# Token halves at a tile's end, and a later fetch of the first rows of sums, in a two-layer hybrid diffusion kernel

## What is computed

```python
DEPTH, SEQ, CTX_LEN, D_MODEL = 2, 512, 256, 1024
PEER_HEADS, N_KEYS, N_EXPERTS, PEER_TOPK, PEER_BLOCK = 8, 128, 128 * 128, 16, 128

def peer(h, w_q, sub_keys, u_tab, v_tab):
    b, L, _ = h.shape
    q = (h @ w_q).reshape(b, L, PEER_HEADS, 2, D_HALF)
    scores = jnp.einsum("blhtd,htkd->blhtk", q, sub_keys)
    ...                 # top 16 of both key halves, top 16 of their sums
    gate = jax.nn.softmax(top_s.astype(jnp.float32), axis=-1).astype(h.dtype)
    ...
    def experts(args):  # blocks of 128 tokens, 8 heads x 16 experts each
        xt, it, gt = args
        act = jax.nn.gelu(jnp.einsum("tkd,td->tk", u_tab[it], xt))
        return jnp.einsum("tk,tkd->td", gt * act, v_tab[it])
    ...

def reference(...):
    for l in range(DEPTH):
        mod = (silu_c @ w_mod[l] + b_mod[l])[:, None, :]   # conditioning
        ...             # context: projection, bidirectional scan, final states
        ...             # latent: projection, pooling, bidirectional scan, mixing
        x = layer_norm(DEEPNORM_ALPHA * x + g1 * mix, ln_g[l, 0], ln_b[l, 0])
        h2 = x * (1 + sc2) + sh2
        x = layer_norm(DEEPNORM_ALPHA * x + g2 * peer(h2, ...), ln_g[l, 1], ln_b[l, 1])
        if not last:
            ...         # the same mixing and peer() for the context tokens
    return x
```

## Time and profile before

| | us |
|---|---|
| median of 3 runs | 4668.28 |
| lowest and highest run | 4664.34, 4676.31 |
| the profiled execution's own time | 4667.22 |
| its span in the trace | 4665.4 |

### The profile page before, as it was taken

One profiled execution on the slowest core, in us unless ns is written; L12 is line 12 of the kernel. 1 busy time (PEld: TensorE's weight loads), 2 busy tenths in 40 slices (PEclk: granted clock), 3 DMA queues, 4 the chain that ended last, 5 costly groups with the idle time before them and its releaser, 6 DMA issues. The chain is left out here.

```text
span 4665.4 us, 48881 instructions
## 1 busy us (share of the span) xinstructions
PE 3434.4 (74%) x15768; PEld 1728.3 (37%) x15768; DVE 3191.9 (68%) x6618; ACT 1543.8 (33%) x3799; POOL 2058.5 (44%) x1555
## 2 busy tenths in 40 slices
PE   7898889897799886555777557888997555655554
PEld 6586224332575333111333114767632111111111
DVE  5465887664766767766766776686666677777775
ACT  4442344343442225222222323474222222222221
POOL 0173444543123554555444551034355555555554
PEclk9899999999899989777789788999998777777778
DMA  5647999999647999999999995263699999999998
GB/s 212 218 158 298 410 410 395 420 423 393 232 161 272 422 417 398 409 421 421 398 425 425 391 412 211 101 204 109 236 423 413 416 412 423 414 408 414 411 418 361
DMA packets 276276, 1622.97 MB, mean 348 GB/s; under 512 B 47074, under 2 KB 61218, under 8 KB 87717
## 3 DMA queue, kind: packets, MB, share of 16 engines
q0 software_dynamic: 184320, 1342.26, 69.6%
q1 hardware_dynamic: 91700, 277.59, 16.3%
HBM read 1598.40 MB, written 21.33 MB: 347 GB/s over the span
## 5 line engine op out<-in xcount | busy, mean ns | idle before, releaser
L2727 PE MATMUL banks<-arena 128*64 128x512 f32 x5120 | 1569.3, 748 | 1003.2 <-ACT arena L2483 1001.8
L2193 POOL DMA_INDIRECT arena<-in_experts,arena x1280 | 1527.0, 1193 | 1660.0 <-PE banks L2727 1408.3
L2316 DVE CUSTOM_DVE_ANT_0 arena<-arena,token_copies 128x1024 f32<-128x1024 f32 x1280 | 1638.4, 1297 | 741.7 <-DMA arena<-in_experts,arena 681.6
L2727 PEld LDWEIGHTS banks<-arena 128*64 128x64 f32 x5120 | 377.1, 163 | 1983.4 <-ACT arena L2483 1357.0
L2476 ACT ACTIVATE arena<-arena 128x2 f32<-128x2 f32 x640 | 131.2, 205 | 1747.2 <-DVE arena L2316 1746.1
L2483 ACT ACTIVATE arena<-arena 128x64 f32<-128x64 f32 x1280 | 376.0, 340 | 298.8 <-POOL arena L2014 257.9
L303 POOL TENSOR_TENSOR wide_low<-wide_blocks,wide_high 128x1024 fp32r<-128x1024 f32 x88 | 219.1, 2513 | 277.7 <-ACT wide_high L292 233.3
L2540 PE MATMUL banks<-arena,wide_blocks 128*128 128x512 f32 (+3 forms) x960 | 307.0, 467 | 3.5 <-ACT arena L2345 2.1
L1025 POOL TENSOR_TENSOR arena<-arena 128x1024 f32<-128x1024 f32 x20 | 43.3, 2191 | 530.4 <-POOLq L853 479.5
L2617 PE MATMUL banks<-arena,wide_blocks 128*128 128x512 f32 x576 | 277.2, 619 | 0.0
L347 PE MATMUL banks<-activation_a,wide_high 128*128 128x256 f32 (+1 forms) x768 | 255.9, 333 | 23.8 <-DVE arena L1462 10.4
(11 more groups left out here) (268 smaller groups left out, 4789.0 us busy)
## 6 DMA issues: line engine op xcount, KB each, us to landing
wide_blocks<-in_wide SPq DMA_DIRECT2D x186, 1024.0 KB, 6.0
arena<-cum_rows SPq DMA_DIRECT2D x80, 256.0 KB, 3.8
arena<-in_experts,arena POOLq DMA_INDIRECT x1280, 11.1
pre_scan<-arena SPq DMA_DIRECT2D x16, 256.0 KB, 7.3
arena<-pre_scan SPq DMA_DIRECT2D x16, 256.0 KB, 5.2
residual<-in_tokens SPq DMA_DIRECT2D x6, 512.0 KB, 6.4
arena<-mod_rows SPq DMA_DIRECT2D x6, 512.0 KB, 8.5
norm_rows<-in_keys SPq DMA_DIRECT2D x3, 1024.0 KB, 6.5
```

The lines of the kernel that those rows point to most:

```text
L2193: pool.indirect_dma_start(out=v.ring[:, g % RING], out_offset=None, in_=io["experts"], in_offset=bass.IndirectOffsetOnAxis(ap=c.idx[:, u % ...
L2316: last = nc.vector.tensor_tensor_reduce(out=u_row, in0=u_row, in1=k.copies[:, n % NJ], scale=1.0, scalar=0.0, op0=ALU.mult, op1=ALU.add, a ...
L2727: mm = nc.tensor.matmul(k.ps[j * QUAD:(j + 1) * QUAD, a + half], v.lhs[:, g % 4, j], v.ring[:, (g * NJ + j) % RING, D + half * BANK:D + (h ...
```

## The change

**Row order.** At the seven tile ends, the last unit of the old tile and the first of the new one (14 of 80 units) take all eight rows of half 0 first and then all eight of half 1 (`row_of`). The other units are as before. Masks, gather indices, token copies and matmul targets follow `row_of`; the flags that start and stop an accumulation go by half. The copies of half 0 are made after the fourth group of the last unit, where VectorE has done the old tile's half 0, and those of half 1 after the last group. In the border units the two rows of a group therefore belong to the same half, and all four matmuls of a group write the same 64 output partitions.

**Rows of sums.** SyncE issues conditioning blocks up to half of the stage's count plus three, instead of two plus three, before it fetches the four tiles of rows, and ScalarE's two `unit_decays` come two turns later.

```diff
@@ -859,7 +859,7 @@
             if mods:
-                load_wides(k, sp, w0 + 2 + WIDE_SLOTS)
+                load_wides(k, sp, w0 + mods.count // 2 + WIDE_SLOTS)
             if rows:
@@ -908,8 +908,9 @@
                 mods.take(act, i)
-                if rows and i - turns // 2 in range(EARLY_UNITS):
-                    unit_decays(k, act, v, i - turns // 2, 0, 0, i - turns // 2, row0)
+                n = i - turns // 2 - 2
+                if rows and n in range(EARLY_UNITS):
+                    unit_decays(k, act, v, n, 0, 0, n, row0)
             if rows and not mods:
@@ -2074,6 +2075,17 @@
     dot_at = lambda g: FIRST + 22.0 + ROW * g
+    def row_of(u, n):
+        border = (u % PEER_HEADS == 0 and u) or (u % PEER_HEADS == PEER_HEADS - 1 and u < UNITS - 1)
+        return (n % RANKS, n // RANKS) if border else (n // NJ, n % NJ)
+    def first_of_half(u, n):
+        return all(row_of(u, x)[1] != row_of(u, n)[1] for x in range(n))
+    def last_of_half(u, n):
+        return all(row_of(u, x)[1] != row_of(u, n)[1] for x in range(n + 1, TOPK))
     PRE, ITEM = proj_at(N) + 8.0, (8.0 if short else 13.0)
@@ -2084,7 +2096,8 @@
     kept_before = lambda e: sum(1 for x in range(e) if keep_of(x) == keep_of(e))
-    copy_at = lambda n: FIRST + 13.0 + 3.0 * n if n < 2 * NJ else dot_at(n // (2 * NJ) * PEER_HEADS * TOPK - 1) + 5.0
+    copy_at = lambda n: (FIRST + 13.0 + 3.0 * n if n < 2 * NJ else
+                         dot_at(n // (2 * NJ) * PEER_HEADS * TOPK - 1 - (RANKS if n // 2 % NJ == 0 else 0)) + 5.0)
     first_two = (2 if ahead else 1) if short else 1 if not ahead else NT
@@ -2179,6 +2192,11 @@
         def _(pool):
+            def row_index(u, n):
+                q, j = row_of(u, n)
+                return c.idx[:, u % 4, q, j:j + 1]
             def gather():
@@ -2192,7 +2210,7 @@
                             out=v.ring[:, g % RING], out_offset=None, in_=io["experts"],
-                            in_offset=bass.IndirectOffsetOnAxis(ap=c.idx[:, u % 4, n // NJ, n % NJ:n % NJ + 1], axis=0),
+                            in_offset=bass.IndirectOffsetOnAxis(ap=row_index(u, n), axis=0),
                         ).then_inc(k.landed[g % RING].sem, 16)
@@ -2307,14 +2325,15 @@
                         yield dot_at(g)
-                        if u % PEER_HEADS == 0 and n < NJ:
-                            dve.wait_ge(k.copy_ready.sem, k.copy_ready.at(t * 2 * NJ + 2 * n + 2))
+                        j = row_of(u, n)[1]
+                        if u % PEER_HEADS == 0 and first_of_half(u, n):
+                            dve.wait_ge(k.copy_ready.sem, k.copy_ready.at(t * 2 * NJ + 2 * j + 2))
                         dve.wait_ge(k.landed[g % RING].sem, r0 + 16 * (g // RING + 1))
...
                         last = nc.vector.tensor_tensor_reduce(
-                            out=u_row, in0=u_row, in1=k.copies[:, n % NJ], scale=1.0, scalar=0.0,
+                            out=u_row, in0=u_row, in1=k.copies[:, j], scale=1.0, scalar=0.0,
                             op0=ALU.mult, op1=ALU.add, accum_out=c.act_in[:, g % 32:g % 32 + 1])
@@ -2446,15 +2465,15 @@
 
-            def copies(t):
-                for j in range(NJ):
+            def copies(t, part):
+                for j in part:
                     for half in range(2):
...
                         if t >= 1:
-                            act.wait_ge(k.dots.sem, b0["dots"] + t * PEER_HEADS * RANKS)
+                            act.wait_ge(k.dots.sem, b0["dots"] + t * PEER_HEADS * RANKS - (RANKS // 2 if j == 0 else 0))
                         nc.scalar.copy(k.copies[:, j, half * BANK:(half + 1) * BANK],
@@ -2463,7 +2482,7 @@
                 c.take_gates(act, 0)
-                yield from copies(0)
+                yield from copies(0, range(NJ))
                 yield FIRST + 13.0 + 8.0
@@ -2480,15 +2499,16 @@
                         for j in range(NJ):
-                            last = nc.scalar.activation(v.lhs[:, g % 4, j], c.masked[:, q * NJ + j], ACT.Copy,
+                            rank, part = row_of(u, q * NJ + j)
+                            last = nc.scalar.activation(v.lhs[:, g % 4, j], c.masked[:, rank * NJ + part], ACT.Copy,
                                                         scale=c.gel[:, a + j:a + j + 1])
...
                             c.softmax(act, u + 2)
-                    if u % PEER_HEADS == PEER_HEADS - 1 and t + 1 < NT:
-                        yield from copies(t + 1)
+                        if u % PEER_HEADS == PEER_HEADS - 1 and t + 1 < NT and q % (RANKS // 2) == RANKS // 2 - 1:
+                            yield from copies(t + 1, [q // (RANKS // 2)])
                     if u % PEER_HEADS == 1 and t >= 1:
@@ -2684,13 +2704,13 @@
 
-            def copies(t):
-                if t == 1:
+            def copies(t, part):
+                if t == 1 and 0 in part:
                     pe.wait_ge(k.s_copied.sem, nth(k.s_copied, N))
-                if t == first_two and ahead and short:
+                if t == first_two and ahead and short and 0 in part:
                     pe.wait_ge(k.pre["evac"].sem, pre0["evac"] + ITEMS)
-                for j in range(NJ):
+                for j in part:
                     for half in range(2):
@@ -2724,19 +2744,24 @@
                             for j in range(NJ):
+                                n = q * NJ + j
+                                part = row_of(u, n)[1]
                                 mm = nc.tensor.matmul(
-                                    k.ps[j * QUAD:(j + 1) * QUAD, a + half], v.lhs[:, g % 4, j],
+                                    k.ps[part * QUAD:(part + 1) * QUAD, a + half], v.lhs[:, g % 4, j],
                                     v.ring[:, (g * NJ + j) % RING, D + half * BANK:D + (half + 1) * BANK],
-                                    start=(first and q == 0), stop=(final and q == RANKS - 1), skip_group_check=True)
+                                    start=(first and first_of_half(u, n)), stop=(final and last_of_half(u, n)),
+                                    skip_group_check=True)
                         mm.then_inc(k.slot_free.sem, 1)
...
                             c.spread(pe, u + 1)
+                        if final and t + 1 < NT and q == RANKS // 2 - 1:
+                            yield from copies(t + 1, [0])
                     if final:
...
                         if t + 1 < NT:
-                            yield from copies(t + 1)
+                            yield from copies(t + 1, [1])
 
...
     k.loaded.advance(64)

```

## The result

The changed kernel takes 4716.12 us, the median of nine runs (4689.21 to 4726.12), against 4667.29 us for nine runs of the kernel before. The ratio is 1.0101, its 95% interval 1.0086 to 1.0116: by the ratio 47 us more (40 to 54). I had forecast 4675 and a range up to 4700. The side on which the sum lay was right; the size was not.

What follows compares the result with a forecast made beforehand. The DMA engines were taken as the bound in retrieval. Terms -8 + 9 + 2 + 6 - 2 = +7 us on 4667.2 gave 4674, and 4675 as the profiled execution lies 1 us below the median; range 4652 to 4700.

Steps and rivals of the forecast that it cites:

- the hidden rival: Lengthened groups cost nothing, because matmuls of one half overlap or the queue takes it all: about 4652 us; chance 0.22.
- The third rival: A group's eight weight loads, 163 ns each, no longer run beside the other half's matmuls: about 4710 us; chance 0.06.
- -8: Six latent tile ends: removing the bubbles gives back 8.1 us at best, bounds 0 and 12.3.
- part 1: Bubbles at the seven tile ends: the wait for token copies is covered twice over; removing them gives at most 17.8 us.
- The fourth rival: Half 0's copies come late because TensorE's list reaches them late, and the wait returns: 4680 us; chance 0.04.
- The rival with TensorE as the bound in the latent units: Groups of layers 0 and 1, at half clock: 58 us a unit that now takes 40; 4704 us; chance 0.18.
- the 199 us: TensorE in the 14 border units: 1.78 us more for each of 112 same-half groups at the full clock.
- Context, +9: Context's two border units: 122.6 us of TensorE work in 105, less queue and small gaps: +9 us, +2 to +17.
- Layer 0 at 1825: Layer 0's tile end at 1825 us: 90 us of TensorE work in 90, so the queue covers it.
- At 2515: Layer 0's tile end there: 101 us of TensorE work in 89, less queue and gaps: +2 us, 0 to +8.
- Unit starts, 12 x 0.5 = +6: Latent stages: 12 unit starts with the queue already empty, 0.5 us each: +6 us, 0 to +22.
- Part 3, -2: States stages: two more blocks go before the four tiles of rows, shortening TensorE's 2.71 us wait: -2 us, -2.7 to +1.

Runs made afterwards that it cites:

- the spread kernel: Kernel before, with 112 groups writing one half, one or two in each of the 80 units: 4710.64 us against 4666.85, ratio 1.009.

## Why the prediction was wrong

**The mechanism held.** Same-half groups take 3.65 us at the full clock, as I took them from the wide records (13 of the 112 last 5.2 to 6.6 us, in part at the half clock), and other groups are unchanged. With that the hidden rival is out. The Trainium skill says (TensorEngine Tiling (Array Packing), Key Properties) that different tiles of the array can load weights and multiply in parallel. The runs agree, with the other side of it: eight records over two column halves take 1.94 us, eight in one half 3.65 us and four in one half 1.93 us. The third rival, loads no longer hidden, is out: eight records with their eight loads take 3.65 us, which is the 0.456 a record of the earlier trace rows and nothing on top. The Trainium skill's rule that loads overlap only where the row group differs (TensorE: Matmul & The Clock Gate, The mechanism) is not what these groups show, since all of them load all 128 rows. The same section of the Trainium skill also lets loads into the background weight buffer run ahead of running matmuls, which would fit; no run here shows whether that is what happens.

**The gain held.** -8 and the 5.5 inside the context's term, 13.5 together, against a measured 10 (4 to 15) in the kernel with the new order and other targets. The copies are covered twice over, as part 1 said: 1.3 us of waits are left. The fourth rival, late copies of half 0, is out with that.

**The rival with TensorE as the bound in the latent units did not occur.** It needed units at the half clock throughout. The clock rose, from 0.71 to 0.90 in layer 1's first border unit and from 0.83 to 0.92 at 1823 us, and the eight border units at the four tile ends without a projection last 40.9 to 44.2 us.

**The step that failed is what covers the 199 us.** I took 11.1 us of landing time for 6 us of queue that a late slot may use up, set that credit against the groups in the first two terms below, and in the third let only the groups next to a unit start pay. The three come to +17 us; the runs show 60 us for the late groups alone:

- *Context, +9.* Its deficit before any discount was 17.6, and 17.1 is what the three units lost. The gathers of the first of the two units went from 13.5 to 7.3 us until landing, so the queue was in fact used up, and the time was lost all the same: 21.2 us in the two units, of which 4.1 came back in the one behind. The lower half of my bounds (+2 to +17) was made of discounts that did not exist. Over the two units themselves the same sum is 85.7 + 28.5 = 114 us of work in 94, a deficit of 20, which is what was lost in them.
- *Layer 0 at 1825, "90 us of work in 90, so the queue covers it", 0.* Measured +11. I added both units before dividing. The projection lies in the last unit alone: there 35.9 us of 47 were busy, 14.2 come on top, which is 50 in 47, and the first unit of the new tile has room that comes too late. At 2515 it is 35.4 + 14.2 = 49.6 in 46: I had +2 and it is +9, where the deficit undiscounted was 12.
- *Unit starts, 12 x 0.5 = +6.* At the four tile ends without a projection the trace has +4.6, +1.2, +3.7 and +5.6, 15 in all with their bubbles won back, and the kernel that delays only these loses 20. That is 0.32 us a group. The bounds (0 to 22) held it and the value taken was low: the spread kernel shows that a single late group in the middle of a unit pays as well, 0.38 us on average.

Even so 50 in 47 is 3 us, not the 14 by which that unit grew. Where the trace can be read, the rest goes with the order of the lists. ScalarE takes the copies in its one list, and half 0's copies now stand between two groups of the old tile. At 1825 they are late, since TensorE reaches them late, and GELU and masks of the next group are queued behind them:

```profile
1824.66 0.58 ACT L2477 COPY token_copies<-banks 128x512 f32<-128x512 f32 x1 [5.83 <-PE banks L2724]
1826.44 0.59 ACT L2477 COPY token_copies<-banks 128x512 f32<-128x512 f32 x1 [1.19 <-PE banks L2724]
1826.92 0.21 ACT L2495 ACTIVATE arena<-arena 128x2 f32<-128x2 f32 x1
1827.20 0.59 ACT L2503 ACTIVATE arena<-arena 128x64 f32<-128x64 f32 x2
```

Behind the context's tile end the same loop closes on GpSimd. ScalarE's copy for half 1 started at 801.65 us after 9.36 us of waiting, the masks of two groups behind it went at 804.20 and 804.95, and TensorE, with copies and projection between, ended the new tile's first group at 808.5. GpSimd:

```profile
799.14 0.94 POOL L2211 DMA_INDIRECT arena<-in_experts,arena  x1 [0.30 <-issue]
800.10 1.91 POOL L2015 TENSOR_TENSOR arena<-fold,arena 128x1024 f32<-128x1024 f32 x1
808.76 0.97 POOL L2211 DMA_INDIRECT arena<-in_experts,arena  x1 [6.75 <-PE banks L2749]
```

Here the DMA rate fell to 6 and 11 GB/s in two slices of 1.4 us. This hole is not new. It is the bubble of the kernel before, shortened but not closed:

```profile
798.83 1.70 POOL L2193 DMA_INDIRECT arena<-in_experts,arena  x1 [10.56 <-PE banks L2727]
```

With the new order and the halves in turn among the targets, GpSimd's longest wait for a group at this place is this:

```profile
791.92 1.94 POOL L2211 DMA_INDIRECT arena<-in_experts,arena  x1 [4.09 <-PE banks L2748]
```

So the late groups also took back a part of what the earlier copies had won. ScalarE's waits for TensorE's copies rose from 72.8 to 119.0 us over the run. How much of the 47 us this loop makes, no run tells: the kernel with the new order and other targets has 102.4 us of such waits and gains, so the loop alone costs nothing as long as TensorE is on time; and the old order with same-half targets, where no copy stands between two groups of a tile, loses 60. I read it as a way in which the lateness travels, not as a cause of its own; that is argued, not shown.

**Part 3, -2.** Measured 0 to +13 for that part alone. The wait stands at whichever block comes behind the four tiles of rows, 2.71 us before and 4.06 us in that kernel; I had the later blocks' spare time at 0.5 us and did not charge it. In the full change the wait is 0.96 us at 155.38 and this:

```profile
164.91 1.51 PE L482 MATMUL banks<-wide_blocks,cond_silu 128*32 128x256 f32 x12 [3.67 <-DMA wide_blocks<-in_wide]
```

I had said "another of below 1 us". So this term was mis-sized as well, by 2 us or more; beside the 60 us of the late groups it decides nothing.

By its own marks: copy waits below 15 us, right; groups of 3.4 to 3.9 us, right; 114 us for the context's two units, they took 115.8, but that is luck, since I had set the 105 us of my window against it and the two units took 94.6 before, so they grew by 21.2 us and not by 9; about 371 GB/s, it was 353; no latent border unit above 46 us, wrong: the last units at 1825 and 2515 last 60.9 and 58.4. (They took 46.6 and 46.5 before, and the first units behind them, 49.9 and 49.1 now, took 50.9 and 48.3; I had overlooked that all four stood above my mark already.)

**What stays open.** A second buffer for the token copies would win the bubble with the old order of rows. It was not tried: the copies lie in a part of on-chip memory that this layout fills. Earlier copies alone were worth 4 to 15 us, and I would expect no more from it. And a late group costs 1.2 us in the context's border units (19.0 / 16), nothing that can be measured in its other units, and 0.2 to 0.5 where no projection runs beside, by kernel (11.0 / 48, 20 / 64 and 24.7 / 46). TensorE's idle time accounts for the first two; for the third I have only the sizes.

## What to carry to other kernels

Before the order of a loop is changed, see which output partitions the matmuls that follow each other then write: narrow ones run side by side only while they use different columns of the array, and a new order can double them without one more instruction. Count a full engine by the stretch in which it is full, not over that stretch and its empty neighbour, and do not take the time that transfers spend in flight for a credit: where the slots of the ring come free through the full engine, it had to be paid back here. Take a wait for what the DMA engines, the bound here, lose in it: 10 us and not the 56 that VectorE stood.

## What the runs showed of the hardware

- Eight float32 records of 512 columns, 64 output partitions wide, take 1.94 us at the full clock when they alternate between two column halves and 3.65 us in one half, with their eight weight loads hidden in both cases.
- A ring of eight slots with 11.1 us from issue to landing does not take up single groups that are 1.78 us late: 0.38 us of each comes out at the end, on average over 112 of them.
- A busier TensorE had the higher granted clock in all five windows above, 0.71 to 0.90 in layer 1's first, so part of a lengthening is paid back there: 199 us were added to the groups at full clock, and their busy time rose by 135.
